# Feed-forward of a two-part transformer program on one core: weights up rounded in halves, the last rows' turn beside the first chunk, sums three to a bank, a second place for high parts

## The reference, cut to what matters

```python
for l in range(2):
    mod = (silu(c) @ w_ada[l] + b_ada[l])[:, None, :]
    shift_a, scale_a, gate_a, shift_f, scale_f, gate_f = jnp.split(mod, 6, axis=-1)
    h = rms_norm(x) * (1.0 + scale_a) + shift_a
    x = x + gate_a * hybrid_mixer(h, ...)
    h = rms_norm(x) * (1.0 + scale_f) + shift_f
    x = x + gate_f * (jnp.square(jax.nn.relu(h @ w_mlp_up[l])) @ w_mlp_down[l])
```

## Time and profile before

| | us |
|---|---|
| median of 3 runs | 4109.55 (4108.57 to 4112.57) |
| the profiled execution | 4113.81 |
| its span | 4112.3 |
| granted TensorE clock over it | 0.947 of full speed |
| feed-forward of layer 0, up 0 to the end of down 15 | 750.98 to about 1581.4 |
| feed-forward of layer 1, up 0 to the end of down 15 | 2267.63 to about 3008.1 |

### The profile page before, as it was taken

How to read it: one execution, slowest core, us unless ns; L and a number is a source line. 1 busy time by engine, 2 the same in 40 slices (tenths; PEclk the granted TensorE clock), 3 DMA queues, 4 the chain that set the end, 5 groups by cost and what they waited for, 6 DMA issues and landing times. The chain is left out here.

```text
span 4112.3 us, 42120 instructions
## 1 busy us (share of the span) xinstructions
PE 3758.9 (91%) x16939; PEld 2438.3 (59%) x16939; DVE 1884.7 (46%) x3396; ACT 1002.2 (24%) x1791; POOL 684.1 (17%) x654
## 2 busy tenths in 40 slices
PE   5999799799999998999889899999998987999994
PEld 3666454577777776666454688888764544333331
DVE  5777563355555545777434334434435544000003
ACT  2444222322222222443223222222221311111111
POOL 0111000100000000111000011001010001555554
PEclk9999799899999999999899999999999998999997
DMA  5000640022222222000410111111220021877633
GB/s 200 24 30 19 208 136 31 28 72 72 73 73 74 73 92 103 31 24 14 161 66 26 41 51 42 52 43 50 72 75 2 21 88 50 346 282 248 221 93 138
DMA packets 225635, 364.51 MB, mean 89 GB/s; under 512 B 54297, under 2 KB 156179, under 8 KB 213153
## 3 DMA queue, kind: packets, MB, share of 16 engines
q1 hardware_dynamic: 177024, 239.55, 17.3%
q0 software_dynamic: 47232, 121.75, 8.4%
q10 hardware_dynamic: 1184, 0.53, 0.0%
HBM read 518.97 MB, written 44.04 MB: 137 GB/s over the span
## 5 line engine op out<-in xcount | busy, mean ns | idle before, releaser
L223 PE MATMUL psum<-arena_r,arena_r 128*128 128x512 f32 x4096 | 1335.9, 406 | 41.7 <-POOL weight_ring_r L1629 18.8
L223 PE MATMUL psum<-arena 128*128 128x128 f32 (+10 forms) x4312 | 904.5, 379 | 50.0 <-DVE arena L2930 14.9
L223 PEld LDWEIGHTS psum<-arena_r,arena_r 128*128 128x128 f32 x4096 | 793.2, 194 | 238.9 <-issue 44.1
L223 PEld LDWEIGHTS psum<-arena 128*128 128x128 f32 (+3 forms) x4312 | 551.1, 190 | 375.8 <-issue 231.1
L1670 DVE TENSOR_TENSOR arena<-arena,psum 128x512 f32<-128x512 f32 x512 | 343.3, 686 | 232.0 <-PE psum L223 231.6
L223 PE MATMUL psum<-weight_ring_r,arena_r 128*128 128x512 f32 x1024 | 423.7, 414 | 0.0
L223 PE MATMUL psum<-arena_r,weight_ring_r 128*128 128x512 f32 x1024 | 401.5, 392 | 0.0
L223 PE MATMUL psum<-arena,weight_ring 128*128 128x512 f32 x768 | 341.8, 605 | 19.7 <-DVE arena L2122 12.6
L1629 POOL TENSOR_TENSOR weight_ring_r<-weight_ring,arena_r 128x2048 fp32r<-128x2048 f32 x32 | 152.2, 4755 | 1246.7 <-ACT arena_r L1594 1246.7
L3042 PE MATMUL psum<-arena 128*64 128x512 f32 x1536 | 343.1, 599 | 4.9 <-DMA arena<-in_expert_w_gate,be_i 3.4
L1661 DVE TENSOR_TENSOR arena_r<-arena,arena_r 128x512 fp32r<-128x512 f32 x128 | 88.7, 693 | 519.0 <-ACT arena_r L1622 519.0
(11 more groups left out here) (374 smaller groups left out, 3400.6 us busy)
## 6 DMA issues: line engine op xcount, KB each, us to landing
weight_ring<-in_w_mlp_up SPq DMA_DIRECT2D x32, 1024.0 KB, 6.3
weight_ring<-in_w_mlp_down SPq DMA_DIRECT2D x32, 1024.0 KB, 4.9
arena<-in_w_ada SPq DMA_DIRECT2D x24, 1024.0 KB, 7.2
arena<-in_w_ada SPq DMA_DIRECT2D x40, 512.0 KB
arena<-in_w_in SPq DMA_DIRECT2D x6, 2048.0 KB, 18.1
tmp_ys<-arena SPq DMA_DIRECT2D x24, 512.0 KB
arena<-in_w_out SPq DMA_DIRECT2D x2, 4096.0 KB, 22.9
arena<-tmp_mixed SPq DMA_DIRECT2D x16, 512.0 KB, 3.3
```

The source lines that it names most:

```text
L223: i = self.nc.tensor.matmul(out, lhs, rhs, start=start and n == 0, stop=stop and n == len(pairs) - 1)
```

## The change

Six things, all in the two layers:

1. **Units.** Two accumulators, and three places in `ps[7]`, one for each unit of a chunk. TensorE takes the units up after down parts 7, 12 and 15. VectorE copies the three results out together, after part 0 of the next chunk's down projection.
2. **Up weights in halves.** `up_hi` and its low part are made in two blocks of 128 hidden columns; ScalarE rounds a block as soon as the chunk before has used it (`up_last`), between the squares of up parts 1 and 2, and after part 3. Chunk 0 takes its parts in another order (`up_part`): both blocks of tokens 0 to 511, then both of 512 to 1023.
3. **Start.** The first two parts of up 0 stand in `pe_output`, one before and one after the turn of the last tile. ScalarE squares the last tile before it scales the last but one, and VectorE normalises it before it makes the `lo` of the last but one.
4. **Down weights of chunk 0** are prepared ahead of the first up results.
5. **A second place of high parts.** The down weights of chunk 15 have their high part in the memory of `up_hi`, and ScalarE's wait for them is for up 15 in place of down 14.
6. **Mixer weights.** Three semaphores in place of `up_in`, each waited for at its first use. `wq_up` lies in the memory of `up_hi`; in layer 1 it and `w_gate` are therefore loaded after the last store of x.

```diff
-    V.w, V.acc, V.bias = A.take(KC, P), A.take(P), A.take(P)
+    V.w, V.acc, V.bias = A.take(KC, P), [A.take(P) for _ in range(2)], A.take(P)
...
+def unit_column(u):
+
+    return P * (u % 3)
...
-    if u > 0:
-        E.wait_ge(S_.ada_pe.at("unit", l, u - 1))
+    acc = V.acc[u % 2]
+    if u > 1:
+        E.wait_ge(S_.ada_pe.at("unit", l, u - 2))
...
-        E.wait_ge(S_.ada_dve.at("unit_take", l, u - 1))
+    if u >= 3:
+        E.wait_ge(S_.ada_dve.at("unit_take", l, 3 * (u // 3) - 1))
     if ada_part(u // 4)[1] == 2:
-        ins = k.mm(k.ps[7][:, 0:P], [(k.c(K_ONE), V.acc)])
+        ins = k.mm(k.ps[7][:, first:first + P], [(k.c(K_ONE), acc)])
...
-    E.wait_ge(S_.ada_pe.at("unit", l, u))
+    first = unit_column(u)
+    E.wait_ge(S_.ada_pe.at("unit", l, min(3 * (u // 3) + 2, UNITS[-1])))
...
+def sp_up_weights(k, l):
+    nc, S_, V, d = k.nc, k.S, k.mix, k.d
+    nc.sync.dma_start(V.w_gate[0:GR], d["w_gate_up"][l]).then_inc(*S_.gate_up_in.dma(l))
+    nc.sync.dma_start(V.wq_up, d["w_q_up"][l].rearrange("(k p) n -> p k n", p=P)).then_inc(*S_.q_up_in.dma(l))
...
-    nc.sync.dma_start(V.wq_up, d["w_q_up"][l].rearrange("(k p) n -> p k n", p=P)).then_inc(*S_.up_in.dma())
-    nc.sync.dma_start(V.w_gate[0:GR], d["w_gate_up"][l]).then_inc(*S_.up_in.dma())
+    if l == 0:
+        sp_up_weights(k, l)
...
-        E.wait_ge(S_.up_in.at(l), S_.mix_act.at("h1", l, 0))
+        E.wait_ge(S_.gate_up_in.at(l), S_.mix_act.at("h1", l, 0))
...
+            if t == 0:
+                E.wait_ge(S_.q_up_in.at(l))
...
+        if t == 0:
+            E.wait_ge(S_.kv_up_in.at(l))
...
     pe_turn_normed(k, l, NT - 2)
+    pe_up_part(k, l, 0, 0)
     pe_turn_normed(k, l, NT - 1)
+    pe_up_part(k, l, 0, 1)
...
+    act_normed(k, l, NT - 1)
     act_normed_turned(k, l, NT - 2)
-    act_normed(k, l, NT - 1)
     act_normed_turned(k, l, NT - 1)
...
-    dve_normed_turned(k, l, NT - 2)
+    dve_high_turned(k, l, NT - 2)
     dve_normed(k, l, NT - 1)
+    dve_low(k, l, NT - 2)
     dve_normed_turned(k, l, NT - 1)
...
-    V.up_hi, V.down_hi = k.rounded(A.take(KC, 256)), k.rounded(A.take(2, D))
+    up, down = A.take(KC * 256), A.take(2 * D)
+    V.up_hi, V.down_hi = k.rounded(shaped(up, (KC, 256))), [k.rounded(shaped(w, (2, D))) for w in (down, up)]
...
+def up_part(n, j):
+
+    return (j % 2, j // 2) if n == 0 else (j // 2, j % 2)
+
+
+def up_last(n, blk):
+
+    return 2 + blk if n == 0 else 1 + 2 * blk
...
+    if l + 1 < DEPTH:
+        sp_up_weights(k, l + 1)
...
+        E.wait_ge(S_.ff_pe.at("up", l, n - 1, up_last(n - 1, blk)))
+    k.nc.scalar.activation(V.up_hi[:, :, at(blk)], V.up_w[up_slot(n)][:, :, at(blk)], ACT.Copy).then_inc(*S_.ff_act.up("up_hi", l, n, blk))
...
+def down_high(k, n):
+    return k.ff.down_hi[1 if n == FFC - 1 else 0]
+
+
+def act_down_high(k, l, n):
+    S_, E, V = k.S, k.act, k.ff
+    E.wait_ge(S_.ff_dve.at("gated", l, n))
+    if n == FFC - 1:
+        E.wait_ge(S_.ff_pe.at("up", l, n, 3))
+    elif n > 0:
+        E.wait_ge(S_.ff_pe.at("down", l, n - 1, NT - 1, 1))
+    k.nc.scalar.activation(down_high(k, n), V.down_w[down_slot(n)], ACT.Copy).then_inc(*S_.ff_act.up("down_hi", l, n))
...
+    act_down_high(k, l, 0)
...
-        if 0 < n < FFC:
-            act_up_high(k, l, n)
-        if n > 0:
-            m = n - 1
-            E.wait_ge(S_.ff_dve.at("gated", l, m))
-            if m > 0:
-                E.wait_ge(pe.at("down", l, m - 1, NT - 1, 1))
-            s.activation(V.down_hi, V.down_w[down_slot(m)], ACT.Copy).then_inc(*out.up("down_hi", l, m))
+        if n > 1:
+            act_down_high(k, l, n - 1)
...
+                for blk in range(2):
+                    if n + 1 < FFC and j == up_last(n, blk):
+                        act_up_block(k, l, n + 1, blk)
...
+    for blk in range(2):
+        E.wait_ge(S_.ff_act.at("up_hi", l, n, blk))
+        here = (slice(None), slice(None), at(blk))
+        k.nc.gpsimd.tensor_tensor(V.up_lo[up_slot(n)][here], w[here], V.up_hi[here].bitcast(F32), ALU.subtract).then_inc(*S_.ff_pool.up("up_lo", l, n, blk))
...
+    dve_down_weights(k, l, 0)
     for n in range(FFC + 1):
-        if n > 0:
+        if n > 1:
             dve_down_weights(k, l, n - 1)
...
+                if j == 0 and m > 0 and l + 1 < DEPTH:
+                    for u in unit_range(m - 1):
+                        dve_ada_unit_take(k, l + 1, u)
                 for i, u in enumerate(unit_range(m) if l + 1 < DEPTH else ()):
                     if j == 1 + 5 * i:
                         dve_ada_unit(k, l + 1, u)
-                    if j == min(7 + 5 * i, 15):
-                        dve_ada_unit_take(k, l + 1, u)
...
+    blk, half = up_part(n, j)
+    cols, wc, u = at(half, 512), at(blk), up_use(n) + j
+    E.wait_ge(S_.ff_act.at("up_hi", l, n, blk), S_.ff_pool.at("up_lo", l, n, blk))
+    if n == 0:
+        last = NT - 1 if half else NT // 2 - 1
+        E.wait_ge(S_.out_act.at("hi", l, last), S_.out_dve.at("lo", l, last))
+        if j < 2:
+            E.wait_ge(S_.out_act.at("mT", l, NT - 1, j))
+    if u >= 7:
+        E.wait_ge(ff_bank_read(k, l, u))
+    i = k.split_mm(ff_bank(k, u), [(V.up_hi[:, c, wc], V.up_lo[slot][:, c, wc], V.h_hi[:, c, cols], V.h_lo[:, c, cols]) for c in range(KC)])
...
+        if n > 0 or j > 1:
+            pe_up_part(k, l, n, j)
...
-            if j == 5 + 5 * i:
+            if j == min(7 + 5 * i, 15):
...
+    k.pe.wait_ge(k.S.out_dve.at("gated", l, NT - 1, 1))```

Instructions as they stand in each engine's queue. TensorE at the end of the output stage of layer 0; the rows with `const` are the turns of x rows, 8 for a tile, the rows with `weight_ring` the product with w_out, and `arena_r_49`, `_50` are the high and low part of h, `_55` is `up_hi`:

```order
 L231 MATMUL psum<-const,arena 128x128 x16
 L223 MATMUL psum<-arena,weight_ring 128x512 x16
-L231 MATMUL psum<-const,arena 128x128 x16
+L231 MATMUL psum<-const,arena 128x128 x8
 L223 MATMUL psum<-arena_r_49,arena_r_55 128x512
 L223 MATMUL psum<-arena_r_50,arena_r_55 128x512
```

More of the change, by code:

```diff
@@ L456, in dve_ada_unit @@
             E.wait_ge(E.last)
-        ins = k.nc.vector.scalar_tensor_tensor(V.acc, V.w[:, c, :], k.cond[:, c:c + 1], V.acc if c else V.bias, ALU.mult, ALU.add)
+        ins = k.nc.vector.scalar_tensor_tensor(acc, V.w[:, c, :], k.cond[:, c:c + 1], acc if c else V.bias, ALU.mult, ALU.add)
         ins.then_inc(*(E.up() if c < KC - 1 else S_.ada_dve.up("unit", l, u)))
@@ L475, in dve_ada_unit_take @@
     part, what, n = ada_part(u // 4)
-    E.wait_ge(S_.ada_pe.at("unit", l, u))
+    first = unit_column(u)
+    E.wait_ge(S_.ada_pe.at("unit", l, min(3 * (u // 3) + 2, UNITS[-1])))
     if what == 2:
-        ins = v.tensor_copy(k.gate[:, part, at(4 * n + u % 4)], k.ps[7][:, 0:P])
+        ins = v.tensor_copy(k.gate[:, part, at(4 * n + u % 4)], k.ps[7][:, first:first + P])
     else:
         c = 4 * n + u % 4
-        ins = v.tensor_scalar_add(k.mod[:, l, part, what, c:c + 1], k.ps[7][:, 0:1], float(what))
+        ins = v.tensor_scalar_add(k.mod[:, l, part, what, c:c + 1], k.ps[7][:, first:first + 1], float(what))
     ins.then_inc(*S_.ada_dve.up("unit_take", l, u))
@@ L592, in sp_mixer_weights @@
         E.wait_ge(S_.ff_pe.at("down", l - 1, FFC - 2, NT - 1, 1))
-    nc.sync.dma_start(V.wkv_up, d["w_kv_up"][l]).then_inc(*S_.up_in.dma(l))
+    nc.sync.dma_start(V.wkv_up, d["w_kv_up"][l]).then_inc(*S_.kv_up_in.dma(l))
 def sp_first_x(k, l):
@@ L1433, in dve_normed_turned, with dve_high_turned @@
 def dve_normed_turned(k, l, t):
+    dve_high_turned(k, l, t)
+    dve_low(k, l, t)
+def dve_high_turned(k, l, t):
     S_, E, V = k.S, k.dve, k.outs
@@ L1439, in dve_normed_turned, with dve_low @@
     i.then_inc(*S_.out_dve.up("h0", l, t))
+def dve_low(k, l, t):
+    S_, E, V = k.S, k.dve, k.outs
     E.wait_ge(S_.out_act.at("hi", l, t))
     here = (slice(None), slice(None), at(t))
-    v.tensor_tensor(V.h_lo[here], V.hT[here], V.h_hi[here].bitcast(F32), ALU.subtract).then_inc(*S_.out_dve.up("lo", l, t))
+    k.nc.vector.tensor_tensor(V.h_lo[here], V.hT[here], V.h_hi[here].bitcast(F32), ALU.subtract).then_inc(*S_.out_dve.up("lo", l, t))
 def dve_output(k, l):
@@ L1612, in act_ff @@
             for j in range(4):
-                blk, cols = j // 2, at(j % 2, 512)
+                blk, half = up_part(n, j)
+                cols = at(half, 512)
                 whole, hi = V.u[b][:, blk, cols], V.u_hi[b][:, blk, cols]
@@ L1645, in dve_down_weights @@
     E.wait_ge(S_.ff_act.at("down_hi", l, n))
[L1646 removed]
+    v.tensor_tensor(V.down_lo[down_slot(n)], w, down_high(k, n).bitcast(F32), ALU.subtract).then_inc(*S_.ff_dve.up("down_lo", l, n))
 def dve_ff(k, l):
@@ L1673, in dve_ff, with pe_up_part, pe_up @@
                         dve_ada_unit(k, l + 1, u)
[L1674 to L1678 removed]
+def pe_up_part(k, l, n, j):
     S_, E, V = k.S, k.pe, k.ff
     slot = up_slot(n)
[L1681 to L1687 removed]
+    blk, half = up_part(n, j)
+    cols, wc, u = at(half, 512), at(blk), up_use(n) + j
```

(12 more changed lines are left out.)

21 lines of the change are left out of this document (6 added, 15 removed).

## The result

| | before | changed |
|---|---|---|
| median of 4 runs each, same chip | 4111.03 us (4108.57 to 4112.57) | 3985.16 us (3982.30 to 3986.59) |
| ratio of the two | | 0.9693, 95% interval 0.968 to 0.9705 |
| the profiled execution, and its span | 4113.81, 4112.3 | 3985.03, 3983.7 |
| granted clock over the span | 0.947 | 0.964 |

The prediction was 3977.5 us, range 3955 to 4008: right in sign, 7.7 us too low, inside the range. Between the two profiled spans lie 128.6 us; the prediction's sum was 132.1. In the experiments one of the 12 executions of e7 took 7895.45 us; its ratio is taken without it, and no run shows the cause.

A forecast was written before the change was run, and what follows sets the result against it. TensorE was busy 91% of the span, so gains could only be its idle or slow-clock time. Terms 77.8 + 47.8 + 0 + 6.5 = 132.1 us, off a median of 4109.55, gave 3977.5 us, range 3955 to 4008.

The forecast's parts named there:

- units: Feed-forward chunks with modulation units: TensorE's unit waits and the slow clock behind them mostly go, gaining 77.8 us.
- start of feed-forward, two layers: From the turn of the last tile but one to down 0: waits and slow clock shrink, gaining 47.8 us.
- end of feed-forward: Chunk 15's down weights: both 7.3 us waits stay because of VectorE's queue order, gain 0.
- mixer weights: Kernel start: TensorE's 5.48 us wait for `wkv_up` and slow clock go, gaining 6.5 us, bounds 0 and 8.
- The bound from above, 1.9 a chunk: Third unit of each chunk: late by 1.9 us if its transfer takes 5.56; units then gain only 60 us.
- the forecast of 0.5: Third unit of each chunk: its lateness was taken to cost 0.5 us a chunk, 6.5 us over 13.
- the case for 0.3 of lateness and a sum of 80: Third unit's transfer: weights issued behind it take no bandwidth, so it is late by 0.3 us; units gain 80.
- The rival of 3957: End of feed-forward: the end waits go as well, giving 3957 us; chance 0.05 for 3945 to 3965.
- The decay chain: Kernel start: ScalarE's stand at the second x tile makes this chain gain less than TensorE's 6.5 us.
- that rival: Third unit late by 2.8 us or more, clock falls, units bring 6 to 20 us: 4035 to 4050; chance 0.12 (4005 to 4050).
- Halves as slow as wholes: Unit 0's port conflict stays at full length, making unit 2 late by 2.7 us; no separate chance given.
- a slow transfer that stops VectorE's queue: Unit 2's transfer of about 14 us holds up VectorE's additions and gate product: above 4118 us; slower, chance 0.015.

The follow-up runs named there:

- e7: The kernel before with only the three mixer semaphores in place of one, no load moved: 4104.23 us, ratio 0.9977.
- e2: The changed kernel with two buffers for the units' weights and bias rows: 3973.62 us, ratio 0.9669.
- e6: The kernel before with only the up weights rounded in halves: 4029.81 us, ratio 0.98.
- e3: The changed kernel with a later chunk's up weights issued only after the third unit's transfer has landed: 3979.42 us, ratio 0.9682.
- e8: The changed kernel with the first two up parts moved out of the output stage, behind the last turn: 4003.60 us, ratio 0.973.
- e4: The changed kernel without the second place of high parts and without the late mixer weight loads: 3983.76 us, ratio 0.969.
- e1: The changed kernel with VectorE's gate product and low part for chunk 15's down weights made earlier: 3961.17 us, ratio 0.9637.
- e5: The kernel before with only the unit change (accumulators, bank places, later units), up weights rounded whole: 4088.78 us, ratio 0.9939.

## Why the prediction was right, step by step

| step | predicted us | measured us, profile against profile |
|---|---|---|
| units | 77.8 | 74 |
| start of feed-forward, two layers | 47.8 | 48.6 |
| end of feed-forward | 0 | 0 |
| mixer weights | 6.5 | 8.25 |
| differences between the executions | | -2 |
| sum | 132.1 | 128.6 |

- **Units.** 13 periods of 51.22 - 46.02 give 67.7, the unit of chunk 13 some 6 (from it to the last addition, 101.5 us before and 95.3 now). The mechanism ran as told, almost on its times from the end of the up projection: first unit ended at 8.2 us (8.4 told), second at 15.8 (15.7), third at 24.2 (23.0), asked for at 22.8 (22.7). Two sizes were off. The units' matmuls cost 0.61 a chunk and not 0.4 (e2): 14 x 0.2 = 2.8 us. And the waits for third units cost 0.60 a chunk (e2) where 0.5 was taken: 1.3 us. The step behind that is the third transfer, taken at 3.9 us from one row of a second unit. Before's trace could hardly correct it: there VectorE came to 12 of the 13 third units after the landing, and only the one of the earlier trace rows shows its length, 5.56 us. But 3.9 was not the most that a second unit took there: one had 4.60. In the changed kernel all 13 are waited for, and they take 4.15 on the mean. The bound from above, 1.9 a chunk by 5.56, was too pessimistic; the forecast of 0.5 was a choice between the two bounds and not worked out, so that it came near is in part luck. It was also priced as if a stop cost its own length alone, from 1.02 us idle in a window of 20; that was two stops, of 0.42 and 0.60 us. The clock did stay up behind longer ones (1.51 here), but the cost is 1.6 to 1.7 times the list (e2, e6).
- **What stands behind the third transfer.** The megabyte slows it by 0.3 us (e3); the case for 0.3 of lateness and a sum of 80 fell, and with it what the Trainium skill's rule of ring order (DMA: Bandwidth & Descriptors, section Queues, rings and completion order) would have given.
- **Start of feed-forward.** 71.97 - 47.3 = 24.7 in layer 0 and some 23.9 in layer 1, for 23.9 each. The wait left is 0.53 and not 1.2. e6 and e8 split the 48.6 into 23.1 for the halves, 20.4 for the covering products and 5.1 for the rest.
- **End.** The wait stayed because VectorE's order sets it. e4 shows that the place alone is worth nothing, e1 that VectorE's move is worth 9.5 and 9.1 us. The rival of 3957 had the right price for the waits and was wrong on what takes them away.
- **Mixer weights.** 8.25 in the first comparison (the turn of the last tile but one, 738.07 and 729.82), 8.1 over all profiled runs: above my 6.5 and at the upper bound. The decay chain that I thought would hold the start back does not. In layer 1 the late loads cost nothing (e4), as forecast. The -2 of the table is 1.7 us between the two feed-forward stages and 1.4 behind the second, less 1.0 gained inside it; what set them is open.
- **Rivals.** No clock fell at the third unit: its stops were 1.5 us at most. e5 is the nearest case to that rival, with stops of 2.5 to 3.4 us; the clock fell behind 9 of 13, and a fall cost about 1.7 us of the 3.2 that I gave it. The rival's 6 to 20 us for all units fit the 15 of e5's profiled execution and not the 26.5 of its median. Halves as slow as wholes, and a slow transfer that stops VectorE's queue, did not occur.
- **The median.** 7.7 us too low: 3.3 from the sum, and the rest from taking 4.3 off for the profiled run of before being above its median, while the changed kernel's profiled run lies at its median.
